# Expert stage: base expert 2 takes the overflow tiles' weight slot, and its weights are asked for in the routing stage

## What is computed

```python
g_sel = argmax(u @ w_rg + b_rg)                       # 1 of 4 groups of experts
e_prob = softmax((u @ w_re + b_re)[g_sel])            # the group's 8 experts
top_p, top_i = top_k(e_prob, 2)                       # 2 experts for each token
hid = silu(u @ w_gate_e[e]) * (u @ w_up_e[e])         # 256 wide
y = h + sum over the 2 experts of weight * (hid @ w_down_e[e])
```

## Time and profile before

| | |
|---|---|
| median of 3 runs | 2438.6 us (2435.96 to 2442.25) |
| the profiled execution | 2439.31 us |
| its span, first to last instruction | 2437.4 us |
| TensorE busy | 2071.8 us, 85% |
| mean granted clock of TensorE | 0.919 |
| DMA, mean | 252 GB/s; the packets of 614.90 MB |

### The profile page before, as it was taken

The page is one execution under the profiler, slowest core; times in us unless marked ns, Lnnn a source line. Parts: engine busy times, 40 slices in busy tenths (PEclk is TensorE's granted clock), DMA queues, the critical chain, the costliest instruction groups (busy, mean ns, idle before and its releaser), DMA issues. The chain is left out here.

```text
span 2437.4 us, 33696 instructions
## 1 busy us (share of the span) xinstructions
PE 2071.8 (85%) x13747; PEld 1264.7 (52%) x13747; DVE 521.7 (21%) x1081; ACT 246.4 (10%) x647; POOL 107.8 (4%) x124
## 2 busy tenths in 40 slices
PE   7999999999989999977777788999974577877763
PEld 7887677777766666634444445763332223332321
DVE  2544122234231222211111111110022111111112
ACT  0001111111001212201010001000010000000000
POOL 0000000000000000000000000000002112121211
PEclk8999999989989999989899988999986788888886
DMA  7664643322243333369999998442247999999998
GB/s 259 192 176 146 239 183 135 121 87 104 87 149 106 106 112 103 129 240 413 412 410 411 411 408 342 150 145 107 104 183 315 408 416 411 415 415 392 398 415 338
DMA packets 149543, 614.90 MB, mean 252 GB/s; under 512 B 31780, under 2 KB 68917, under 8 KB 111733
## 3 DMA queue, kind: packets, MB, share of 16 engines
q1 hardware_dynamic: 107310, 545.19, 57.4%
q0 software_dynamic: 22800, 45.07, 5.2%
q10 hardware_dynamic: 19288, 22.55, 2.9%
HBM read 702.95 MB, written 39.60 MB: 305 GB/s over the span
## 5 line engine op out<-in xcount | busy, mean ns | idle before, releaser
L517 PE MATMUL bank<-ut,wring 128*128 128x320 f32 x1408 | 385.4, 435 | 1.1 <-PEq L205 1.1
L517 PEld LDWEIGHTS bank<-ut,wring 128*128 128x128 f32 x1408 | 268.5, 192 | 111.2 <-issue 3.2
L806 PE MATMUL bank<-ut,wring 128*128 128x320 f32 x1024 | 299.6, 439 | 0.8 <-DVE ncum L1050 0.6
L806 PEld LDWEIGHTS bank<-ut,wring 128*128 128x128 f32 x1024 | 190.8, 192 | 74.8 <-issue 9.7
L2034 PE MATMUL bank<-wdn,par 128*32 128x512 f32 x512 | 87.1, 813 | 108.9 <-issue 108.3
L2005 PE MATMUL bank<-wgu,arena 128*32 128x512 f32 x1024 | 123.1, 622 | 0.8 <-DVE arena L2085 0.8
L1476 PE MATMUL bank<-wring,arena 128*128 128x512 f32 x256 | 118.4, 606 | 3.1 <-DVE arena L1513 1.6
L680 DVE RECIPROCAL selmask<-selmask 128x320 f32<-128x320 f32 x30 | 64.5, 2149 | 201.4 <-ACT selmask L654 201.4
L1375 DVE TENSOR_REDUCE wring<-bank 128x1 f32<-128x512 f32 x32 | 22.1, 691 | 331.5 <-PE bank L1197 331.5
L2034 PEld LDWEIGHTS bank<-wdn,par 128*32 128x32 f32 x512 | 18.2, 132 | 140.4 <-issue 139.3
L1476 PEld LDWEIGHTS bank<-wring,arena 128*128 128x128 f32 x256 | 46.1, 190 | 74.6 <-issue 70.1
(11 more groups left out here) (418 smaller groups left out, 2307.4 us busy)
## 6 DMA issues: line engine op xcount, KB each, us to landing
wgu<-in_w_gu SPq DMA_DIRECT2D x128, 1024.0 KB, 16.7
wdn<-in_w_dn SPq DMA_DIRECT2D x32, 2048.0 KB, 24.5
wring<-in_w_proj SPq DMA_DIRECT2D x44, 1024.0 KB, 4.8
arena<-in_kv_k SPq DMA_DIRECT2D x64, 640.0 KB, 9.7
arena<-in_kv_v SPq DMA_DIRECT2D x64, 640.0 KB, 16.7
wring<-in_w_gate SPq DMA_DIRECT2D x32, 1024.0 KB, 5.1
wring<-in_w_merge SPq DMA_DIRECT2D x32, 1024.0 KB, 4.8
wring<-in_kv_k SPq DMA_DIRECT2D x32, 640.0 KB, 15.0
```

What stands on the lines that cost most here:

```text
L517: last = nc.tensor.matmul(m.bank[:, 2 + s % 2, 0:T], m.wring[:, s, k * P:(k + 1) * P], m.ut[:, k, :], start=(k == 0), stop=(k == KD - 1))
L806: last = nc.tensor.matmul(m.bank[:, 6 + n % 2, 0:T], m.wring[:, n % 3, k * P:(k + 1) * P], m.ut[:, k, :], start=(k == 0), stop=(k == KD - 1))
```

## The change

The gu of base expert 2 goes into `wgu_x`, and its dn into `wdn_x`. SyncE issues the gu in route_stage, in four pieces, as soon as `lg_done` says that `ut` (in the same memory) has been read. It issues the dn as its first instruction in experts_stage, since `wdn_x` holds tables of the routing until that ends. The first overflow tile's weights come into the slot only when b2 is done with it: GpSimd's load_gu(0), which stood right behind the first gather, stands behind the tile ("base", 2) and waits for its gu_done; load_dn(0) waits for its dn_done. `share` puts all overflow tiles behind b2: b0 b1 b2 m0 b3 m1 b4 b5 m2 b6 m3 b7 m4 b8 and so on, 20 overflow tiles as before, in the same order as before from tile 42 on. From b3 on the base experts use the two slots in turn again (b3 follows b0 in slot 0, b4 follows b1 in slot 1). SyncE's list in experts_stage becomes: dn of b2, gu of b3, gu of b4, gu of b5, dn of b3, gu of b6, dn of b4, ... Group 8 (m0 to m3) is now transposed behind first(b2). Nothing that is computed changes.

```diff
+THIRD = 2
 def share(n):
-    return min(NX, (n * NX + NE // 2 - 1) // (NE - 3))
+    return min(NX, (max(n - THIRD, 0) * NX + NE // 2 - 1) // (NE - 3 - THIRD))
+def slot(n):
+    return n if n < THIRD else (n + 1) % 2
+def turn_of(n):
+    return (n - 1) // 2 if n > THIRD else 0
+def before_in_slot(n):
+    return n - 3 if n < THIRD + 3 else n - 2
@@ route_stage, SyncE
+            sp.wait_ge(lg_done, 1)
+            for c in range(4):
+                sp.dma_start(e.wgu_x[:, 4 * c:4 * c + 4, :].rearrange("p k n -> p (k n)"),
+                             a["w_gu"][THIRD * P:(THIRD + 1) * P, c * DM:(c + 1) * DM]).then_inc(r_in, 16)
@@ experts_stage, SyncE (load_gu and load_dn: n - 2 becomes before_in_slot(n), n % 2 slot(n))
-            for n in range(2, NE + 2):
+            sp.dma_start(e.wdn_x[:, :, :].rearrange("p f n -> p (f n)"), a["w_dn"][THIRD * P:(THIRD + 1) * P, :]
+                         ).then_inc(e.moved, 16)
+            for n in range(THIRD + 1, NE + 2):
                 if n < NE:
                     load_gu(n)
-                if n >= 4:
+                if n >= THIRD + 3:
                     load_dn(n - 2)
@@ experts_stage, GpSimd
             def load_gu(x):
-                if x:
-                    pool.wait_ge(gu_done, AT["more", x - 1] + 1)
+                pool.wait_ge(gu_done, AT["more", x - 1] + 1 if x else AT["base", THIRD] + 1)
...
             def load_dn(x):
-                if x:
-                    pool.wait_ge(dn_done, AT["more", x - 1] + 1)
+                pool.wait_ge(dn_done, AT["more", x - 1] + 1 if x else AT["base", THIRD] + 1)
...
             gather(0)
-            load_gu(0)
             n = 1
             for i, (kind, x) in enumerate(ORDER):
...
+                if (kind, x) == ("base", THIRD):
+                    load_gu(0)
@@ experts_stage, TensorE, first(i)
+                w = e.wgu_x[:, :, :] if kind == "more" or x == THIRD else e.wgu[:, slot(x), :, :]
+                elif x == THIRD:
+                    pe.wait_ge(e.r_in, 64 + 16 * 4)
@@ second(i)
+                        pe.wait_ge(e.moved, 96 + 16)
```

More of the change, by code:

```diff
@@ L1587, in __init__ @@
         self.gu_in = [[sem(f"gu_in{s}_{c}") for c in range(4)] for s in range(2)]
+        self.r_in, self.moved = sem("r_in"), sem("moved")
         self.dn_in = [sem(f"dn_in{s}") for s in range(2)]
 def load_base(eng, e, a, n):
-    s = n % 2
+    s = slot(n)
     for c in range(4):
@@ L1627, in c @@
             return ec[0:rows, at:at + n]
-        r_in, un_ready, moved, fold_done, rs_ready = (
-            sem("r_in"), sem("un_ready"), sem("moved"), sem("fold_done"), sem("rs_ready"))
+        r_in, moved = e.r_in, e.moved
+        un_ready, fold_done, rs_ready = sem("un_ready"), sem("fold_done"), sem("rs_ready")
         tr_done, kept_a, kept_d, wr_ready = sem("tr_done"), sem("kept_a"), sem("kept_d"), sem("wr_ready")
@@ L1646, in _ @@
             sp.dma_start(e.stack[:, :], a["e_consts"][:, at:at + n]).then_inc(moved, 16)
-            for n in range(2):
+            for n in range(THIRD):
                 load_base(sp, e, a, n)
+            sp.wait_ge(lg_done, 1)
+            for c in range(4):
+                sp.dma_start(e.wgu_x[:, 4 * c:4 * c + 4, :].rearrange("p k n -> p (k n)"),
+                             a["w_gu"][THIRD * P:(THIRD + 1) * P, c * DM:(c + 1) * DM]).then_inc(r_in, 16)
         @block.gpsimd
@@ L1894, in load_gu @@
                     if c < 3:
-                        sp.wait_ge(gu_free, 3 * (n - 2) + c + 1)
+                        sp.wait_ge(gu_free, 3 * before_in_slot(n) + c + 1)
                     else:
-                        sp.wait_ge(gu_done, AT["base", n - 2] + 1)
-                    sp.dma_start(e.wgu[:, n % 2, 4 * c:4 * c + 4, :].rearrange("p k n -> p (k n)"),
-                                 a["w_gu"][n * P:(n + 1) * P, c * DM:(c + 1) * DM]).then_inc(e.gu_in[n % 2][c], 16)
+                        sp.wait_ge(gu_done, AT["base", before_in_slot(n)] + 1)
+                    sp.dma_start(e.wgu[:, slot(n), 4 * c:4 * c + 4, :].rearrange("p k n -> p (k n)"),
+                                 a["w_gu"][n * P:(n + 1) * P, c * DM:(c + 1) * DM]).then_inc(e.gu_in[slot(n)][c], 16)
             def load_dn(n):
-                sp.wait_ge(dn_done, AT["base", n - 2] + 1)
-                sp.dma_start(e.wdn[:, n % 2, :, :].rearrange("p f n -> p (f n)"), a["w_dn"][n * P:(n + 1) * P, :]
-                             ).then_inc(e.dn_in[n % 2], 16)
-            for n in range(2, NE + 2):
+                sp.wait_ge(dn_done, AT["base", before_in_slot(n)] + 1)
+                sp.dma_start(e.wdn[:, slot(n), :, :].rearrange("p f n -> p (f n)"), a["w_dn"][n * P:(n + 1) * P, :]
+                             ).then_inc(e.dn_in[slot(n)], 16)
+            sp.dma_start(e.wdn_x[:, :, :].rearrange("p f n -> p (f n)"), a["w_dn"][THIRD * P:(THIRD + 1) * P, :]
+                         ).then_inc(e.moved, 16)
+            for n in range(THIRD + 1, NE + 2):
                 if n < NE:
                     load_gu(n)
-                if n >= 4:
+                if n >= THIRD + 3:
                     load_dn(n - 2)
@@ L1991, in first @@
                 g = t // 4
[L1992 to L1996, removed]
+                u = e.ut_b[:, g % 2, :, :] if kind == "base" else e.ut_x
+                w = e.wgu_x[:, :, :] if kind == "more" or x == THIRD else e.wgu[:, slot(x), :, :]
+                if kind == "more":
+                    pe.wait_ge(gu_x_in, 16 * (x + 1))
+                elif x == THIRD:
+                    pe.wait_ge(e.r_in, 64 + 16 * 4)
                 pe.wait_ge(ut_ready, 4 * GROUPS.index(g) + 4)
@@ L2002, in first @@
                     q = k % 4
-                    if kind == "base" and q == 0:
-                        pe.wait_ge(e.gu_in[x % 2][k // 4], 16 * (x // 2 + 1))
+                    if kind == "base" and x != THIRD and q == 0:
+                        pe.wait_ge(e.gu_in[slot(x)][k // 4], 16 * (turn_of(x) + 1))
                     last = nc.tensor.matmul(m.bank[q * TW:(q + 1) * TW, i % 2, :], u[:, k, lo:lo + TW], w[:, k, :],
@@ L2022, in second @@
                 pe.wait_ge(hid_ready, i + 1)
-                if kind == "base":
-                    pe.wait_ge(e.dn_in[x % 2], 16 * (x // 2 + 1))
-                    w = e.wdn[:, x % 2, :, :]
-                else:
-                    pe.wait_ge(dn_x_in, 16 * x + 16)
+                if kind == "base" and x != THIRD:
+                    pe.wait_ge(e.dn_in[slot(x)], 16 * (turn_of(x) + 1))
+                    w = e.wdn[:, slot(x), :, :]
+                else:
+                    if kind == "more":
+                        pe.wait_ge(dn_x_in, 16 * (x + 1))
+                    else:
+                        pe.wait_ge(e.moved, 96 + 16)
                     w = e.wdn_x[:, :, :]
```

## The result

| | before | changed |
|---|---|---|
| median, 6 runs each | 2439.26 us (2435.96 to 2445.34) | 2458.96 us (2455.97 to 2464.48) |
| profiled execution, span | 2439.31 us, 2437.4 | 2460.34 us, 2458.5 |
| end of the merge (L1480's last matmul) to the end | 644.1 us | 663.2 us |

The ratio is 1.0080 [1.0063, 1.0096]: 19.7 us slower. The forecast was 2443.0, in 2431 to 2451; it was wrong. The medians in this document are of all runs and the ratios of the fast ones alone; two slow runs of e3_extra_fetch and one of e8_all_three raise their medians by 1.6 and 2.2 us.

What follows compares the result with a forecast made beforehand. It took the expert stage to be paced by weight transfers at 414 GB/s. Idle DMA time: early 25.5 against 15.8 us (9.7 more), late 5.3 less, together + 4.4: 2443.0 us, 8 in 10 for 2431 to 2451.

Steps and rivals of the forecast that it cites:

- The currency: Expert stage: time is bytes over rate plus idle DMA time; bytes are unchanged, so idle DMA time decides.
- the ledger: Sum of idle DMA time, length x (1 - GB/s / 414) per window; before: early 15.8 us, late 6.8.
- no effect: Rival: TensorE's or the receipt's latency paces the tiles, so DMA idle time doesn't count: 2438.6 us, chance 0.08.
- Part 1: Routing's end: b2's gu follows without a break to 1856.5, filling 10.1 of 13.1 idle us.
- Part 2: Routing's end: scatters and read-back of tok_at run beside the new load, 3 us later, bounds 0 and 5.2.
- the border: Between routing and expert stage: idle 13.1 us before, 4.5 forecast, from 1856.5 to 1861.0.
- Part 3: Stage start: b2's dn ahead of the first gather delays it 4 us; with Part 2, TensorE's tiles 7 us late.
- Part 4: Stage start, order in which slots come free: idle stretches of 4.5, 10 and 11 us.
- Second hole: Between gather(0) and the next gu, which needs first(b0)'s first quarter: 10 us idle.
- third: Around 1911 to 1921: TensorE stands at first(m0) for m0's gu, queues empty: 11 us idle, bounds 5 and 12.
- Part 5: Later stage: dips come from turns behind overflow tiles; of 6.8 us, 5.3 back, 1.5 left for m4.
- the late dips stay: Slower rival: dips come from TensorE waiting for dn with an overflow tile behind; + 9.7, 2448.3 us, chance 0.29.

Runs made afterwards that it cites:

- e3: Kernel before plus four unread pieces (4.19 MB) fetched into wgu_x in the routing, m0's gu waiting for them: 2451.35 us, 1.0028.
- e8: Changed kernel with half of b2's gu fetched in the routing, the rest and b2's dn behind the first gather, overflow tiles from behind b4: 2442.29 us, 0.9988.
- e1: Changed kernel with overflow tiles m4, m5 and m6 standing one base tile further on: 2452.27 us, 1.0037.
- e12: Kernel before with another tile order alone, 20 overflow tiles over 23 base tiles against 29: 2452.18 us, 1.0036.
- e13: As e8, with the 20 overflow tiles spread over 27 base tiles: 1.0007.
- e16: Changed kernel with share alone altered: m0 behind b3, 20 overflow tiles over 29 base tiles: 1.0014.
- e15: Kernel before with share alone altered, 20 overflow tiles over 31 base tiles: 1.0001.
- e14: As e13, with no piece of b2's gu fetched before the first gather has landed: 1.0007.
- e7: Changed kernel with SyncE waiting for the first gather's landing before it issues b2's dn: 2455.09 us, 1.0036.
- e4: Changed kernel with b2's gu issued at the head of the expert stage, not in the routing: 2451.36 us, 1.0030.
- e6: Changed kernel with the overflow tiles beginning behind b4 instead of b2: 2440.77 us, 0.9998.
- e5: Changed kernel with m0's gu one place earlier in GpSimd's list, ahead of group 1's gather: 2450.53 us, 1.0034.
- e11: As e8, with the 20 overflow tiles over 22 base tiles instead of 25: 2457.44 us, 1.0065.
- e2: Kernel before with only the changed kernel's share, so its tile order; slots and loads as before: 2443.67 us, 0.9994.

## Why the prediction was wrong, by its own steps

**The currency held.** For before, changed and e1 to e12 the stage is the ledger's sum plus 621 us, within 3 (618.5 to 622.8, with 10.1 taken off for e3's extra bytes). The rival "no effect", that DMA idle time is not what is paid in, falls. For e13 to e16 it is 625 to 631, of which the longer way from the last `second` explains 4 in e13, e14 and e16. e15 has no longer way, but its engines fall idle around the last `second` itself (234, 130, 0 and 12 GB/s in the four windows from 2396 to 2404, 6.2 us by the ledger's formula, some 5 of it behind the ledger's end); the rest of its 10 us stays open.

**Part 1, right but for one stretch:** 410 and 422 GB/s in the gap that the fetch was to fill, but 111 from 1850 to 1854, so that it ended at 1860, not 1856.5.

**Part 2, its size wrong.** 3 us were taken, with 5.2 as the worst. The stage's first gather came 7.3 us later, in e3 7.0. The bound was worked out from a scatter beside the old loads (5.6); the last scatter and the read-back took 8.8 each up to the next instruction. So the border loses 7.3, not 4.5.

**Part 3, right:** gather(0) takes 2.9 us longer, 3.1 by e7, for 4 forecast. With part 2, TensorE starts 10.3 later from the merge (+69.2 to +79.5), not 7.

**Part 4, right.** Second hole 9.2 in the ledger for 10, third 11.0 for 11, each for the reason given: e4 fills the second with a transfer queued there, e6 removes the third by moving m0, and e5 over half of it by one place in a list.

**Part 5, the step that failed.** "So of 6.8 I expect 5.3 back, with 1.5 for m4." It was +6.0 instead of -5.3: 11.3 us of the 13.2 by which the ledger's +17.6 exceeds the forecast's +4.4 (2.8 are the border; 0.9 the other way, mostly since before's early part is 16.6 by two profiles and 15.8 in the forecast). The step counted turns that follow overflow tiles, one by one. The list it counted from, "m1, m4, b7, b11", had the two turns that mattered in it, but out of their order (b7 comes right before m4), and gave them 1.5 us together. The runs showed in its place that the turn behind b7, m4 and its own turn in a row leave 28 us without a base load, a hole of 9 us (gone in e1), and that a denser order makes holes of its own (e11, e12). How the 6 us divide isn't settled: e1 takes only 3.4 of them out of the ledger, and 6.4 out of the stage. The rival "the late dips stay" named that density, and priced it as no gain where it was a loss of 6 in the ledger.

In time, this step is less sure than in the ledger. Taking the hole away brings some 5 to 10 us by the ratios (e1). But the same order without the moved slot costs nothing that can be seen (e2, 0.9994 [0.9979, 1.0009]). It doesn't bring the forecast's 5.3 us either: those would be 0.9978, just outside.

**Unseen in the forecast:** that the start of before varies. It lost 1.8 us there in one profile and 6.7 in the other, and three kernels with the same first tiles lost 4.3 to 7.1. What sets that isn't settled.

**Where the 10.1 us went.** At the border 5.0 were gained; the second hole (9, but 2.7 in e4) took more than that back. Taking the slot for b2 put m0 where the third hole opens, 11 us, and brought the order with the late 6. The scatters' delay is part of what border and second hole lose. No run shows a gain from the early fetch; e8, the best, is at 0.9988 [0.9971, 1.0005] and can't be told from before.

## What to carry to other kernels

In a stage paced by transfers, look beyond the gap you fill: ask what the fetched slot's former user now waits for, and what the small transfers that open the stage have to pass. When a tile is moved, write down the whole new order and read off for each slot the time from one freed load to the next against what is queued; two turns with an overflow tile between them, or a denser stretch, show there. Take the kernel before twice before a hole of some 5 us in one profile enters a sum.

## What the runs showed of the hardware

- Small scatters and their read-back took longer beside a bulk load, and for some us the load moved fewer bytes. In the 4 us behind the last scatter, the changed kernel's engines were 93% busy and moved 111 GB/s; in three other profiles of kernels with the early fetch the like stretch had 174 to 250 GB/s at a share of 0.84 to 1.08. The chain of scatter, read-back and gather was 8.9 us longer. Small scatters beside a load don't do this in every case: while four of the six were issued beside the old loads, from 1841 to 1846 in the kernel before, the engines moved 442 GB/s at a share of 1.04. What sets the slow stretch isn't shown.
- A gather whose rows are all out of range moves nothing, and under full queues its completion still takes 9.1 to 20.6 us (9.1 to 18.9 for the unused gu of the kernel before, 20.6 for m14's in the changed one, 2244.3 to 2265.0), as against 2.6 to 4.7 for the three issued in or just behind its dips (2.6 for m14's at 2216.9, where the engines moved 238 GB/s). The Trainium skill (DMA: Bandwidth & Descriptors, Latency and other measured facts) gives HBM's access latency as 2 us at high load; the wait here is up to ten times that. I argue that the rest is the transfers queued ahead; no run here tells it apart.
